# The second modulation's products by VectorE instead of TensorE, with weight buffers of their own

## The reference, cut to what matters

```python
mod = (silu(c) @ w_mod + b_mod)          # 6 rows of 1024
sh1, sc1, g1, sh2, sc2, g2 = split(mod, 6)
h = rms_norm(x, norm1_g) * (1 + sc1) + sh1
q_a, k_a, v_a, q_b, k_b, v_b = split(h @ w_in)      # 1024 x 2304
... head norms, rotary positions, two attentions, merge ...
x = x + g1 * merged
h2 = rms_norm(x, norm2_g) * (1 + sc2) + sh2
x = x + g2 * swiglu(h2)
```

## Time and profile before

| | us |
|---|---|
| median of 3 runs | 2682.34 (2680.24 to 2683.26) |
| the profiled execution, its own time | 2682.12 |
| its span, first to last instruction | 2680.3 |
| TensorE busy in it | 2469.3 (92%) |
| VectorE, ScalarE, GpSimd busy | 1621.1, 1061.1, 359.8 |

### The profile page before, as it was taken

The page is one execution under the profiler, slowest core; times in us unless marked ns, Lnnn a source line. Parts: engine busy times, 40 slices in busy tenths (PEclk is TensorE's granted clock), DMA queues, the critical chain, the costliest instruction groups (busy, mean ns, idle before and its releaser), DMA issues. The chain is left out here.

```text
span 2680.3 us, 42340 instructions
## 1 busy us (share of the span) xinstructions
PE 2469.3 (92%) x15597; PEld 2129.4 (79%) x15597; DVE 1621.1 (60%) x2701; ACT 1061.1 (40%) x2101; POOL 359.8 (13%) x507
## 2 busy tenths in 40 slices
PE   4799979988969799999999989997897999999998
PEld 2689877777859688888888889995795888878886
DVE  3523237776764977777677942007529777756677
ACT  1422235555641433333344432124435544444443
POOL 2566312221110200000000010003203000000001
PEclk8899989999979899999999999997898999999999
DMA  8233320000032132333275431110131444377463
GB/s 288 94 111 118 117 52 3 1 1 1 1 125 80 71 103 91 118 102 102 99 271 177 154 123 32 48 32 13 47 127 63 157 146 157 130 253 254 133 187 116
DMA packets 189033, 288.15 MB, mean 108 GB/s; under 512 B 11704, under 2 KB 109948, under 8 KB 188540
## 3 DMA queue, kind: packets, MB, share of 16 engines
q1 hardware_dynamic: 188860, 285.84, 31.9%
HBM read 219.46 MB, written 67.34 MB: 107 GB/s over the span
## 5 line engine op out<-in xcount | busy, mean ns | idle before, releaser
L378 PE MATMUL ps<-w_hi,ht_hi 128*128 128x256 f32 x1744 | 504.3, 289 | 18.5 <-DVE w_lo L363 9.8
L379 PE MATMUL ps<-w_lo,ht_hi 128*128 128x256 f32 x1744 | 498.5, 286 | 0.0
L380 PE MATMUL ps<-w_hi,ht_lo 128*128 128x256 f32 x1744 | 498.4, 286 | 0.0
L378 PEld LDWEIGHTS ps<-w_hi,ht_hi 128*128 128x128 f32 x1744 | 338.6, 194 | 35.4 <-DVE w_lo L363 11.7
L379 PEld LDWEIGHTS ps<-w_lo,ht_hi 128*128 128x128 f32 x1744 | 338.6, 194 | 0.0
L380 PEld LDWEIGHTS ps<-w_hi,ht_lo 128*128 128x128 f32 x1744 | 338.2, 194 | 0.0
L363 DVE TENSOR_TENSOR w_lo<-stage,w_hi 128x2048 fp32r<-128x2048 f32 x31 | 73.7, 2377 | 220.9 <-ACT w_hi L359 220.9
L1696 PE MATMUL ps<-ff_b_hi,ff_a_hi 128*128 128x512 f32 x448 | 174.5, 390 | 2.6 <-DVE ff_b_lo L1684 1.4
L1698 PE MATMUL ps<-ff_b_hi,ff_a_lo 128*128 128x512 f32 x448 | 174.3, 389 | 0.0
L1697 PE MATMUL ps<-ff_b_lo,ff_a_hi 128*128 128x512 f32 x448 | 174.3, 389 | 0.0
L1454 PE MATMUL ps<-ht_hi,swiglu_w_hi 128*128 128x512 f32 x352 | 138.2, 393 | 10.1 <-DVE tmp L1964 7.7
(11 more groups left out here) (361 smaller groups left out, 5748.4 us busy)
## 6 DMA issues: line engine op xcount, KB each, us to landing
ff_a_raw<-ff_act_dram SPq DMA_DIRECT2D x112, 256.0 KB, 2.8
stage<-w_in SPq DMA_DIRECT2D x23, 1024.0 KB, 5.2
swiglu_a_raw<-swiglu_act_dram SPq DMA_DIRECT2D x77, 256.0 KB, 3.0
stage<-w_mod SPq DMA_DIRECT2D x16, 1024.0 KB, 5.5
ff_stage<-w_ff SPq DMA_DIRECT2D x16, 1024.0 KB, 5.4
ff_act_dram<-ff_act_sums SPq DMA_DIRECT2D x16, 1024.0 KB, 4.3
ff_act_dram<-ff_acts SPq DMA_DIRECT2D x16, 768.0 KB, 5.7
swiglu_stage<-w_up SPq DMA_DIRECT2D x11, 1024.0 KB, 5.2
```

What stands on the lines that cost most here:

```text
L378: pe.matmul(bank, a, wh[:, k, :], start=(k == 0), stop=False)
L379: pe.matmul(bank, a, wl[:, k, :], start=False, stop=False)
L380: mm = pe.matmul(bank, b, wh[:, k, :], start=False, stop=(k == KT - 1))
```

## The change

VectorE multiplies a piece's weights (128 partitions x 8 x 256) in place by `silu(c)`, each partition's eight values spread over 256 columns (`modx_dve_mul`), and reduces over the eight (`modx_dve_part`: the input is read with a step of one row of the buffer, 640 floats, or of 256 floats for the last two pieces). TensorE keeps only the sum over the partitions (`modx_pe_sum`), now with a column of -0.5 as weights, which VectorE's last step undoes by a factor of -2. The pieces 0 to 13 land in two buffers, `mod_w2`, that lie in columns of `v_nat` which panels 7 and 8 write later; pieces 14 and 15 land in `stage`. A table (`MODX`) says behind which row tile each step stands: the product behind the squares of tile 1, the reduction behind tile 2, TensorE's sum behind tile 4, and so on. TensorE's nine panels are straight code, with no loop.

```diff
+    mod_w2 = [at(f"mod_w2_{i}", [KT, KVW], F32, nat + NT * D * 4 + 10 * KVW * 4)[:, :, A_KV + i * PN:A_KV + (i + 1) * PN] for i in range(2)]
...
         def sync_x(sp):
-            for p in range(8):
+            def load(m):
+                sp.dma_start(mod_slot(m), mod_panel(m)).then_inc(mod2_in[m % 2], 16)
...
+            def finish(m):
+                sp.wait_ge(modx_row, m + 1)
+                sp.dma_start(mod_flat(m), mod_row[0:1, :]).then_inc(modx_stored, 16)
+                if m < 15:
+                    load_bias(m + 1)
+
+            load(0)
+            load(1)
+            load_bias(0)
+            for p in range(7):
+                load_weights(sp, P_X + p + 2, panel_of(t["w_in"], (p + 2) * PN))
                 for m in (2 * p, 2 * p + 1):
...
+                    if m + 2 < 14:
+                        sp.wait_ge(modx_part, m + 1)
+                        load(m + 2)
+                    if m < 13:
+                        finish(m)
+            sp.wait_ge(w_lo_done, P_O)
+            load(14)
+            finish(13)
+            sp.wait_ge(modx_part, 15)
+            load(15)
+            finish(14)
+            finish(15)
+
+        def mod_slot(m):
+            return mod_w2[m % 2] if m < 14 else stage_up()
...
-                if mods is not None and j >= 4:
+                if mods is not None:
                     mods(j)
...
-        def modx_pe_part(pe, m, first):
-            pe.wait_ge(mod2_landed, 16 * (m + 1))
...
-            for k in range(KT):
-                g = k % 4
-                mm = pe.matmul(ps[32 * g:32 * g + 2, 4, 0:PN], cond[:, :, k], w[:, k, :], start=(k < 4), stop=(k >= 4))
...
+        def modx_pe_sum(pe, m):
+            pe.wait_ge(modx_part, m + 1)
+            if m == 0:
                 pe.wait_ge(tl_done, T_O)
+            pe.matmul(ps[0:1, 5, 0:PN], neg_half[:, 0:1], mod_q[:, :], start=True, stop=True).then_inc(modx_b, 1)
+
+        def modx_dve_mul(dve, m):
+            dve.wait_ge(mod2_in[m % 2], 16 * (m // 2 + 1))
+            dve.tensor_tensor(mod_slot(m), mod_slot(m), bcast(cond[:, 0, :], 2, PN), ALU.mult).then_inc(modx_mul, 1)
 
         def modx_dve_part(dve, m):
+            dve.wait_ge(modx_mul, m + 1)
+            dve.wait_ge(modx_b, m) if m else dve.wait_ge(tl_done, T_O)
+            dve.tensor_reduce(mod_q[:, :], mod_slot(m).rearrange("p k n -> p n k"), AX_X, ALU.add).then_inc(modx_part, 1)
...
-            dve.tensor_tensor(mod_row[0:1, :], ps[0:1, 5, 0:PN], mod_b[0:1, :], ALU.add).then_inc(modx_row, 1)
+            dve.scalar_tensor_tensor(out=mod_row[0:1, :], in0=ps[0:1, 5, 0:PN], scalar=-2.0, in1=mod_b[0:1, :],
+                                     op0=ALU.mult, op1=ALU.add).then_inc(modx_row, 1)
+
+        MODX = {}
+        for p in range(7):
+            MODX[p, 1] = [("mul", 2 * p)]
+            MODX[p, 2] = ([("row", 2 * p - 1)] if p else []) + [("part", 2 * p)]
+            MODX[p, 5] = [("row", 2 * p), ("mul", 2 * p + 1)]
+            MODX[p, 6] = [("part", 2 * p + 1)]
+        MODX.update({(7, 2): [("row", 13)], (7, 3): [("mul", 14)], (7, 4): [("part", 14)], (7, 7): [("row", 14)],
+                     (8, 1): [("mul", 15)], (8, 2): [("part", 15)], (8, 5): [("row", 15)]})
...
+        def modx_pe(pe, p, j):
+            for x, m in MODX.get((p, j + 1), []):
+                if x == "row":
+                    modx_pe_sum(pe, m)
...
-            with pe.Fori(0, 4) as i:
-                for b in range(2):
-                    p = 2 * i + b
-                    for j in rows_pe(pe, P_X + p, (P_X + b) % 2, NT, T_X, D_X + NT * p):
...
+            for p in range(9):
+                for j in rows_pe(pe, P_X + p, (P_X + p) % 2, NT, T_X, D_X + NT * p):
+                    modx_pe(pe, p, j)
```

More of the change, by code:

```diff
@@ L188, in program @@
         skewed, pad_done, bias_in = early("skewed"), early("pad_done"), early("bias_in")
-        mod2_landed, modx_part, modx_q, modx_row, modx_b, modx_out, modx_stored = (
-            early(x) for x in ("mod2_landed", "modx_part", "modx_q", "modx_row", "modx_b", "modx_out", "modx_stored"))
+        mod2_in = [early(f"mod2_in{i}") for i in range(2)]
+        modx_mul, modx_part, modx_row, modx_b, modx_stored = (
+            early(x) for x in ("modx_mul", "modx_part", "modx_row", "modx_b", "modx_stored"))
         ks_hi, ks_lo, kt_tr, kt_a, kt_v = early("ks_hi"), early("ks_lo"), early("kt_tr"), early("kt_a"), early("kt_v")
@@ L230, in sync_x, with load_bias @@
         def sync_x(sp):
-            for p in range(8):
-                for m in (2 * p, 2 * p + 1):
[L234 to L247, removed]
+            def load(m):
+                sp.dma_start(mod_slot(m), mod_panel(m)).then_inc(mod2_in[m % 2], 16)
+            def load_bias(m):
+                sp.dma_start(mod_b[0:1, :], t["b_mod"][0:1, 2 * D + m * PN:2 * D + (m + 1) * PN]).then_inc(modb_in, 16)
+            def finish(m):
[8 more added lines that the diff above has]
+                load_weights(sp, P_X + p + 2, panel_of(t["w_in"], (p + 2) * PN))
+                for m in (2 * p, 2 * p + 1):
+                    if m + 2 < 14:
[12 more added lines that the diff above has]
+            return mod_w2[m % 2] if m < 14 else stage_up()
         def norm_tile(pool, j, before, width, groups=1):
@@ L512, in program @@
         ROPED = 6 * 2 * 3
-        def modx_pe_part(pe, m, first):
-            pe.wait_ge(mod2_landed, 16 * (m + 1))
-            if first:
+        def modx_pe_sum(pe, m):
+            pe.wait_ge(modx_part, m + 1)
+            if m == 0:
                 pe.wait_ge(tl_done, T_O)
-            w = stage_up()
-            for k in range(KT):
-                g = k % 4
-                mm = pe.matmul(ps[32 * g:32 * g + 2, 4, 0:PN], cond[:, :, k], w[:, k, :], start=(k < 4), stop=(k >= 4))
[L523 to L527, removed]
-        def modx_dve_part(dve, m):
[L530 to L535, removed]
+            pe.matmul(ps[0:1, 5, 0:PN], neg_half[:, 0:1], mod_q[:, :], start=True, stop=True).then_inc(modx_b, 1)
+        def modx_dve_mul(dve, m):
+            dve.wait_ge(mod2_in[m % 2], 16 * (m // 2 + 1))
+            dve.tensor_tensor(mod_slot(m), mod_slot(m), bcast(cond[:, 0, :], 2, PN), ALU.mult).then_inc(modx_mul, 1)
+        def modx_dve_part(dve, m):
+            dve.wait_ge(modx_mul, m + 1)
+            dve.wait_ge(modx_b, m) if m else dve.wait_ge(tl_done, T_O)
+            dve.tensor_reduce(mod_q[:, :], mod_slot(m).rearrange("p k n -> p n k"), AX_X, ALU.add).then_inc(modx_part, 1)
         def modx_dve_row(dve, m):
@@ L541, in modx_dve_row, with modx_dve @@
                 dve.wait_ge(modx_stored, 16 * m)
-            dve.tensor_tensor(mod_row[0:1, :], ps[0:1, 5, 0:PN], mod_b[0:1, :], ALU.add).then_inc(modx_row, 1)
+            dve.scalar_tensor_tensor(out=mod_row[0:1, :], in0=ps[0:1, 5, 0:PN], scalar=-2.0, in1=mod_b[0:1, :],
[8 more added lines that the diff above has]
+                     (8, 1): [("mul", 15)], (8, 2): [("part", 15)], (8, 5): [("row", 15)]})
+        def modx_dve(dve, p, j):
+            for x, m in MODX.get((p, j), []):
+                (modx_dve_mul if x == "mul" else modx_dve_part if x == "part" else modx_dve_row)(dve, m)
+        def modx_pe(pe, p, j):
+            for x, m in MODX.get((p, j + 1), []):
+                if x == "row":
+                    modx_pe_sum(pe, m)
         def keys_pe(pe):
@@ L1198, in _ @@
             for q, panel in enumerate(X_PANELS):
[L1199 to L1202, removed]
+                heads_dve(dve, panel, last, P_X + q + 1 if q < 8 else None, NT, 0, D_X + NT * q, 6 + NT * q, n,
+                          lambda j, q=q: modx_dve(dve, q, j))
                 last, n = (panel, n + 1) if panel[0] != "v" else (None, n)
```

## The result

The changed kernel took 2722.46 us (median of 4 runs, 2716.93 to 2728.87) against 2681.29 (2680.03 to 2683.26): a ratio of 1.0154, 95% interval 1.0138 to 1.0171. That is 41 us more; 22 were forecast, the range was 2692 to 2742, and slower had 0.86. It went the forecast way by the forecast mechanism, with one of its terms too small: the reduction over a large step. The favoured case (0.52, with a range of its own of 2692 to 2708) did not come; what came is the rival "slow reduction", in part (0.31), and the stated range holds the time because it reached up to that rival.

A forecast was written before the change was run, and what follows sets the result against it. The prediction took TensorE's queue to bound the nine w_in panels. Products removed (-18.8 us), stalls (+28.5) and clock loss (+12.0) sum to +21.7 us, giving 2704 us, range 2692 to 2742.

The forecast's parts named there:

- forecast mechanism: In the w_in panels, VectorE's product waits behind GpSimd's gain multiply, so TensorE stands before its sum: stalls of 28.5 us.
- The favoured case: Product collides with GpSimd's gain multiply, the reduction's input step is free: 2704 us, own range 2692 to 2708, chance 0.52.
- slow reduction: Rival: the reduction's large input step costs up to 4.6 us, GpSimd's mean falls under the split: up to 2741 us, chance 0.31.
- TensorE's queue is the bound, and the products leave it at 1.175 us each: In the nine w_in panels TensorE is always busy; removing 16 sets of products saves 18.8 us.
- timetable: A panel's expected order of events, counted from E, the start of the last copy of the panel before.
- The product waits for GpSimd's gain multiply: Two-SBUF-input product contends with GpSimd's 4.62 us gain multiply in a panel, so it ends at E + 16.2.
- The sum behind tile 4 turns VectorE's lateness into TensorE's wait: TensorE's even sum waits for the reduction: 4.3 us in panels 1, 4, 5, 6, 8.6 in panel 2, 2.7 in 3.
- lateness of GpSimd: GpSimd's rotary work delays its mean in panel 2 to about E + 5.5 instead of E + 1.2, adding 4.3 us.
- The reduction takes 2.3 us: VectorE's reduction of 128x2048 to 128x256 takes 2.3 us if its 2560-byte input step costs nothing; 4.6 kept as upper bound.
- The earlier landing of w_in costs nothing, the mean starts at E + 1.2: w_in panels land earlier, which only pulls the split forward, at 0 us; GpSimd forms the mean at E + 1.20.
- The clock costs 2.0 us a wait: Behind each of six TensorE stalls the granted clock falls to 0.5, losing 2.0 us (bounds 0 and 2.5), 12.0 in all.
- Side by side: Rival: the product runs beside GpSimd's multiply or gets the ports first; -13.3 us, 2669 us, chance 0.11.

The follow-up runs named there:

- e8: Changed kernel with a chain of eight one-SBUF-input VectorE instructions replacing product and reduction, and e4's table: 2663.1 us, ratio 0.9938 to the kernel before.
- e2: Changed kernel, but the condition is copied once to PSUM and the product reads it there: 2697.7 us, ratio 1.0051 to the kernel before.
- e4: Changed kernel with TensorE's even sum behind tile 6 instead of 4, its row and the odd reduction behind tile 7: 2680.6 us, ratio 0.9987.
- e10: Changed kernel, but the odd piece's reduction stands behind the squares of tile 7 instead of 6: 2703.2 us, ratio 1.0079 to the kernel before.
- e11: Changed kernel, but each piece's reduction reads with another step, 4 to 2560 bytes; ran once, only durations read: about 2.3 us at 4 and 8 bytes.
- e1: Changed kernel, but the reduction takes eight neighbouring values instead of values 2560 bytes apart: 2697.2 us, ratio 1.0045 to the kernel before.
- e6: Kernel before with straight code, the change's two weight buffers and order of DMAs, products still by TensorE: 2680.2 us, ratio 0.9996.
- e3: Changed kernel plus unused filler matmuls in front of TensorE's sum in panels 1 to 6: 2717.3 us, ratio 1.0124 to the kernel before.
- e9: Changed kernel with both the condition read from PSUM and the reduction over eight neighbouring values: 2671.3 us, ratio 0.9967 to the kernel before.

## Why the prediction came out as it did, point by point

- *TensorE's queue is the bound, and the products leave it at 1.175 us each.* Right. Panels without a wait are 24.45 us long (e8), 24.4 in the timetable; before they were 26.8.
- *The product waits for GpSimd's gain multiply.* Right, shown by e2: the time fell by 25 us when its second input left SBUF.
- *The sum behind tile 4 turns VectorE's lateness into TensorE's wait.* Right, shown by e4, which moves the odd reduction too, and by e10, which gives that part alone. The waits lie where they were put, twice as long as forecast in the steady panels (8.4 us for 4.3), 9.5 for 8.6 in panel 2, 3 for 2.7 in panel 3. That the last two came so near is luck: in panel 2 the forecast's lateness of GpSimd was absent and the late squares took its place (above), and in panel 3 the mean ended at E + 4.6, about 1.1 us sooner than forecast, which makes up for most of the dearer reduction.
- *The reduction takes 2.3 us.* This is the term of the sum that failed: it takes 3.76 us. I had no row for a large step and chose the row of the same operation over the Trainium skill's rule, at 0.52 to 0.31. By the Trainium skill (SBUF — State Buffer, "SBUF: two separate sides", on 16-byte lines) an access that leaves a line pays; e11 agrees in the place of the cliff, at 16 bytes, and gives the price, 0.7 us for 1000 values, 1.6 to 1.8 times the time. Directly that is 1.5 us in each of six waits, 9 us. e1, which makes the step free, is the favoured case itself: its stage is 19.7 us longer than before (21.7 forecast), its waits 25.5 (28.5), its median 15 us above.
- *The earlier landing of w_in costs nothing, the mean starts at E + 1.2.* The first half is right alone (e6). The second failed with the reduction: the odd one, too, is longer and delays the last squares by 1.2 us, and then the split stands before the power and holds it. Worth 3.0 us in each of the steady panels. The earlier landing probably has a part in the 1.8 us of the power, since a split at E + 4.1, as before, would have begun behind the power's start at E + 2.8; no run had the reductions with the old order of the loads. The prediction had this step only in its rival "slow reduction" (the mean under the split); e10, which undoes it alone, puts the wait at 5.4 to 5.5 us a panel instead of 8.4 (4.3 + 1.5 = 5.8 by the timetable), and e1, which undoes it with the dear reduction, at 4.0 to 4.3.
- *The clock costs 2.0 us a wait.* Nearly in the sum: 10.7 us against 12.0, but behind waits twice as long. Behind waits near the forecast's 4.3 us it was more, 28.5 x 0.47 = 13.4 us for five waits in e1 and 12.3 for five in e2; 2.5 to 2.7 each, which is the prediction's upper bound. e3 shows that 7 of the 10.7 can be had back. Of the rest 1.6 is panel 2, where the clock fell there too; the remainder stays open.
- *The rival "slow reduction"* had +32 at half the extra cost and +59 at all of it. The extra was two thirds (1.5 of 2.3 us), the result +41. *"Side by side"* was priced at 2669; e9, which makes it so, took 2671.3.

- *A slip in the reading of the rows, without effect:* GpSimd's gain multiply starts 0.2 us behind VectorE's first reduction of squares (160.84 and 160.67 in the earlier trace rows), not before it.

With 3.8 in place of 2.3, and the 3.0 us by which the heads were measured to be late, the prediction's timetable gives, for a steady panel, 4.3 + 1.5 + 3.0 = 8.8 us; 8.4 were measured.

What stays open: the profiles differ by up to 11 us outside the stage, which I didn't follow up. The 3 us between the stage's 38.1 and the medians' 41.2 are within that.

## What to carry to other kernels

Work that is moved off the bounding engine is paid for by that engine's waits, not by the other's busy time: write down, for one period, when the bounding engine asks for each result and when it is ready, and which instruction of a neighbour can hold it up, before choosing the places. VectorE operations with two SBUF inputs beside a busy GpSimd, and reductions whose input steps by 16 bytes or more, are the two to look for; a PSUM operand or accumulator avoids the first, and a chain of scalar-times-tensor-plus-accumulator both. When a wait appears, move it first: here one line of a table was worth 19 us, and two lines as much as the whole change.

## What the runs showed of the hardware that I had not expected

- A VectorE reduction of 128x2048 float32 takes 2.28 us with input steps of 4 or 8 bytes, and 3.57 to 4.12 with 16, 32, 64, 128 or 2560.
- GpSimd's power is not held by VectorE's split when it starts first (5.44 us at 154.19 in e10, with the split from 157.42), but takes 7.24 when the split starts 0.34 us before it: 150.46 and 150.80 above. The 7.24 us end about 5.4 us behind the split's end at 152.75, as if it had begun only then. The other way round, the split of e10 ran its 2.28 us inside the power: the power, though it starts first, does not keep a VectorE operation with two SBUF inputs out for its whole length, as the gain multiply does. For the power, the rule that the prediction quotes (the first holds the ports for its whole instruction) does not come out.
- The same two instructions, product and gain multiply, ran in 6.22 and 4.57 us when both of the product's inputs were in SBUF, and in 2.28 and 4.59 when one was in PSUM.
- Shorter waits did not cost less clock: behind five waits of 4.0 to 7.3 us TensorE worked 28.5 us at the 1.2 GHz level (e1), behind six of 3.0 to 9.5 us 22.7. Behind waits of 1.1 to 2.2 us the clock stayed at 1.00 (panel 3 of e1, e2 and e10).
- A value-per-partition multiply-add of 128x256 into PSUM, each link waiting for the one before, took 0.52 us a link.
